# Unread matmuls in TensorE's waits: convolution, norms and one renumbered PSUM bank in a three-layer network

## The reference

```python
def first_block(...):
    for l in range(2):
        mix = conformer_conv(x, ...) if l == 0 else diff_attention(x, k1, k2, v, ...)
        x = layer_norm(ALPHA * x + mix, ln_mix_g[l], ln_mix_b[l])
        ffn = grouped_moe(x, router_w, router_bias, moe_w_gate[l], moe_w_up[l], moe_w_down[l])
        x = layer_norm(ALPHA * x + ffn, ln_ffn_g[l], ln_ffn_b[l])

def second_block(...):
    h = concatenate([meta, x])
    xn = rms_norm(h, mix_pre_g); proj = xn @ w_in
    y_ssd = ssd_mixer(z, xbc, dt_raw, ...); y_sb = rms_norm(stick_breaking_attention(q, k, v), sb_norm_g)
    h = h + rms_norm(concatenate([y_ssd, y_sb]) @ w_out, mix_post_g)
    xn = rms_norm(h, ffn_pre_g); gu = xn @ w_up
    f = (gelu(causal_dwconv(gu[..., :D_FF])) * gu[..., D_FF:]) @ w_down
    return h + rms_norm(f, ffn_post_g)
```

## Time and profile before

| | us |
|---|---|
| median of 3 runs | 1390.86 |
| lowest and highest | 1387.32, 1391.38 |
| the profiled execution, its own time | 1388.31 |
| its span, first to last instruction | 1386.6 |
| PE busy | 1298.2 (94%) |
| PE weight loads busy | 811.8 (59%) |
| DVE, ACT busy | 385.9 (28%), 262.3 (19%) |
| mean granted clock of PE | 0.966 of full speed |

### The profile page before, as it was taken

One profiled execution on the slowest core, in us unless ns is written; L12 is line 12 of the kernel. 1 busy time (PEld: TensorE's weight loads), 2 busy tenths in 40 slices (PEclk: granted clock), 3 DMA queues, 4 the chain that ended last, 5 costly groups with the idle time before them and its releaser, 6 DMA issues.

```text
span 1386.6 us, 14928 instructions
## 1 busy us (share of the span) xinstructions
PE 1298.2 (94%) x6134; PEld 811.8 (59%) x6134; DVE 385.9 (28%) x851; ACT 262.3 (19%) x579; POOL 35.9 (3%) x62
## 2 busy tenths in 40 slices
PE   7989899999989998999989799999998978999997
PEld 6764444333446864533434288776776867888743
DVE  0014522111141444411211303466323122222101
ACT  1013311000111343200100221411435021000000
POOL 3110000000000000000000000000000000000000
PEclk9999899999999999999999999889999999999999
DMA  9980899999993062999999942212230251544320
GB/s 310 297 266 2 334 386 428 423 426 429 418 384 121 1 242 101 417 423 428 425 426 426 401 182 87 96 61 92 91 121 1 69 174 61 171 133 175 130 91 31
DMA packets 95086, 321.68 MB, mean 232 GB/s; under 512 B 10098, under 2 KB 47510, under 8 KB 80166
## 3 DMA queue, kind: packets, MB, share of 16 engines
q1 hardware_dynamic: 84368, 301.04, 56.0%
q10 hardware_dynamic: 8662, 12.27, 3.0%
q0 software_dynamic: 1984, 7.34, 1.3%
HBM read 316.30 MB, written 4.34 MB: 231 GB/s over the span
## 4 chain that ended last, share of the span: by engine, by line
PE 82%; DMA 9%; DVE 5%; ACT 2%; issue 1%; ACTq 0%; SPq 0%; DVEq 0%; POOLq 0%
PE psum L255 35%; PE psum L1565 12%; PE psum L1598 6%; PE psum L3071 5%; DMA ring<-in_moe_w_up 4%; DMA arena<-in_moe_w_up 4%; PE psum L2870 4%; PE psum L1608 3%; PE psum L623 2%; PE psum L909 2%; PE psum L741 2%; PE psum L1802 2%; PE psum L531 1%; PE psum L1767 1%; PE psum L1224 1%
## 5 line engine op out<-in xcount | busy, mean ns | idle before, releaser
L255 PE MATMUL psum<-xT,ring 128*128 128x256 f32 (+2 forms) x1792 | 409.0, 390 | 3.4 <-DMA ring<-in_a_w_pw 3.4
L255 PEld LDWEIGHTS psum<-xT,ring 128*128 128x128 f32 x1792 | 344.0, 193 | 63.7 <-issue 9.0
L1565 PE MATMUL psum<-ring,arena 128*64 128x512 f32 x672 | 186.1, 599 | 10.1 <-DMA arena<-in_moe_w_up 6.3
L1565 PEld LDWEIGHTS psum<-ring,arena 128*64 128x64 f32 x672 | 60.1, 138 | 100.7 <-issue 100.5
L1446 DVE TENSOR_TENSOR arena<-psum,arena 64x512 f32<-64x512 f32 x32 | 34.2, 1070 | 214.5 <-ACT arena L1509 214.5
L1598 PE MATMUL psum<-ring,arena 128*64 128x512 f32 x384 | 85.0, 595 | 1.3 <-ACT arena L1526 1.3
L3071 PE MATMUL psum<-ring,arena 128*128 128x512 f32 x176 | 75.7, 592 | 0.0
L1565 PE MATMUL psum<-arena 128*64 128x512 f32 x208 | 74.0, 610 | 0.0
L1509 ACT ACTIVATE arena<-psum 64x512 f32<-64x512 f32 x32 | 18.9, 591 | 268.6 <-PE psum L1565 268.6
L1608 PE MATMUL psum<-arena 128*128 128x512 f32 x128 | 59.5, 605 | 0.0
L3071 PEld LDWEIGHTS psum<-ring,arena 128*128 128x128 f32 x176 | 33.4, 190 | 41.7 <-issue 41.6
(11 more groups left out here) (355 smaller groups left out, 1303.6 us busy)
## 6 DMA issues: line engine op xcount, KB each, us to landing
ring<-in_moe_w_down SPq DMA_DIRECT2D x24, 2048.0 KB, 25.5
ring<-in_moe_w_up SPq DMA_DIRECT2D x22, 2048.0 KB, 21.2
ring<-in_moe_w_gate SPq DMA_DIRECT2D x20, 2048.0 KB, 23.1
ring<-in_w_in SPq DMA_DIRECT2D x11, 2048.0 KB, 22.2
ring<-in_w_up SPq DMA_DIRECT2D x22, 1024.0 KB, 7.7
arena<-in_moe_w_gate SPq DMA_DIRECT2D x6, 2048.0 KB, 26.9
ring<-in_w_down SPq DMA_DIRECT2D x5, 2048.0 KB, 7.8
ring<-in_a_w_pw SPq DMA_DIRECT2D x8, 1024.0 KB, 11.0
```

The source lines that it names most:

```text
L255: last = nc.tensor.matmul(dst, lhsT, rhs, start=(n == 0), stop=(n == len(pairs) - 1))
L1565: last = pe.matmul(bank(j)[part, :], tokens[:, k, side * SEATS:side * SEATS + SEATS], weights(u + n, k), start=(k == 0), stop=(k == KC - 1))
```

## The change

`keep_busy(dst, n)` issues n products of `ident` (128 x 128) with 256 columns of `vec` into a PSUM bank from which nobody reads them. It is called in eight places on PE: five products behind `shift_sum` and five ahead of mix0, both into bank 7; three at the start of each `route` into bank 4; and in the norms, into the bank that the transposes are about to take: six ahead of tile 2 in `project_and_turn`, three ahead of each tile in mix1, eight ahead of tile 1 in `ffn_norm0`, fourteen ahead of tile 0 in `pre_norm`, fifteen ahead of tile 1 and eight ahead of tile 0 in `mix_and_turn`. Nine products of `ident` with itself (128 columns) follow the first transposes of the program. In `project_out` the sum of squares of `sqT` moves from bank 4 to a job of its own, so that `w_out` has eleven jobs, every later bank number moves by one and the two halves of the meta rows stand in banks 0 and 1 in their natural order; ACT frees the job's bank with a no-op behind its own result.

```diff
-    ("sb_v", 16), ("w_out", 10),
+    ("sb_v", 16), ("w_out", 11),
...
+    def keep_busy(dst, n):
+
+        for _ in range(n):
+            nc.tensor.matmul(dst[:, 0:2 * P], ident[:, :], vec[:, 0:2 * P], start=True, stop=True)
+
+    def transposes_pe(first, tiles, src, ready=None, busy=None):
...
         for t in tiles:
             n = TILE_N[t]
+            if busy is not None and t in busy:
+                take_bank(j)
+                keep_busy(bank(j), busy[t])
             if ready is not None:
                 ready(t)
...
         def turn(j, t):
-            transposes_pe(j, (t,), lambda t: xhat[t - 1], lambda t: pe.wait_ge(normed, t))
+            transposes_pe(j, (t,), lambda t: xhat[t - 1], lambda t: pe.wait_ge(normed, t), {2: 6})
...
             block.tensor(lambda pe: transposes_pe(first, (1, 2), lambda t: xhat_ffn[t - 1],
-                                                  lambda t: pe.wait_ge(normed, t)))
+                                                  lambda t: pe.wait_ge(normed, t), {1: 8}))
...
             transposes_pe(FJ["conv_xT"], (1, 2), lambda t: x_nat[:, t, :])
+            for _ in range(9):
+                pe.matmul(psum[:, 2 * BANKS - 1, 0:P], ident[:, :], ident[:, :], start=True, stop=True)
...
                         shift_sum()
+                        keep_busy(psum[:, 2 * BANKS - 1, :], 5)
...
+            keep_busy(psum[:, 2 * BANKS - 1, :], 5)
             project_and_turn(FJ["mix0"], unit_at["pw2"], lambda k, t: conv[:, k, (t - 1) * P:t * P], normed[0],
...
         def _(pe):
+            keep_busy(psum[:, BANKS, :], 3)
             all_read_out(pe, J)
...
-                transposes_pe(FJ["mix1"] + 2 * t - 2, (t,), lambda t: xhat[t - 1], lambda t: pe.wait_ge(normed[2], t))
+                transposes_pe(FJ["mix1"] + 2 * t - 2, (t,), lambda t: xhat[t - 1], lambda t: pe.wait_ge(normed[2], t),
+                              {1: 3, 2: 3})
...
         rms_to_T("pre", "pre_xT", lambda t: x_nat[:, t, :], lambda t: xn[:, t, :], xT, "mix_pre_g_2",
-                 ready=lambda t: nc.scalar.wait_ge(normed[3], t) if t else None)
+                 ready=lambda t: nc.scalar.wait_ge(normed[3], t) if t else None, busy={0: 14})
...
-            products(psum[:, BANKS, NEED:L], [(ones[:, :], sqT[:, c, NEED:L]) for c in range(KC)]).then_inc(so_summed_mix_turned, 1)
+            take_bank(SO)
+            products(bank(SO)[:, NEED:L], [(ones[:, :], sqT[:, c, NEED:L]) for c in range(KC)]).then_inc(job_done, 1)
...
-            act.wait_ge(so_summed_mix_turned, MIX_TURNED)
-            act.activation(rms_b, psum[:, BANKS, NEED:L], ACT.Sqrt, bias=eps_cols[:, 1:2], scale=1.0 / D).then_inc(
+            job_ready(act, SO)
+            act.activation(rms_b, bank(SO)[:, NEED:L], ACT.Sqrt, bias=eps_cols[:, 1:2], scale=1.0 / D).then_inc(
                 std_ready, 1)
-            turned_in(FJ["w_out"], mixT)
+            act.wait_ge(std_ready, root)
+            act.nop().then_inc(bank_free[SO % BANKS], 1)
+            turned_in(SO + 1, mixT)
...
             for t in FFN_ORDER:
                 n = TILE_N[t]
+                if t in (0, 1):
+                    take_bank(T + 2 * count[t])
+                    keep_busy(bank(T + 2 * count[t]), 8 if t == 0 else 15)
                 pe.wait_ge(rms_scaled, base + 4 + count[t])
```

More of the change, by code:

```diff
@@ L517, in next_stage @@
         block.gpsimd(meet)
-    def transposes_pe(first, tiles, src, ready=None):
+    def keep_busy(dst, n):
+        for _ in range(n):
+            nc.tensor.matmul(dst[:, 0:2 * P], ident[:, :], vec[:, 0:2 * P], start=True, stop=True)
+    def transposes_pe(first, tiles, src, ready=None, busy=None):
         j = first
@@ L2072, in _, with rms_to_T @@
                                              ALU.mult, ALU.mult).then_inc(scaled, 1)
-    def rms_to_T(name, job_name, src, dst, dstT, gain, pe_first=None, act_between=None, ready=None):
+    def rms_to_T(name, job_name, src, dst, dstT, gain, pe_first=None, act_between=None, ready=None, busy=None):
         first = rms_count[0]
@@ L2080, in rms_to_T @@
             block.scalar(act_between)
-        block.tensor(lambda pe: transposes_pe(FJ[job_name], ALL, dst, lambda t: pe.wait_ge(rms_scaled, first + t + 1)))
+        block.tensor(lambda pe: transposes_pe(FJ[job_name], ALL, dst, lambda t: pe.wait_ge(rms_scaled, first + t + 1),
+                                              busy))
         @block.scalar
@@ L2890, in _ @@
             for t in (1, 2):
-                turn(1, t).then_inc(so_summed_mix_turned, 1)
+                turn(1, t).then_inc(mix_turned, 1)
             for half in range(2):
@@ L2895, in _ @@
                 for c in range(4):
-                    last = pe.transpose(bank(j)[0:META, c * P:c * P + P], mixT[:, 4 * (1 - half) + c, 0:META], ident[:, :])
+                    last = pe.transpose(bank(j)[0:META, c * P:c * P + P], mixT[:, 4 * half + c, 0:META], ident[:, :])
                 last.then_inc(job_done, 1)
@@ L2923, in mix_and_turn @@
         gain_cols = vec[:, VEC_COL["ffn_pre_g_2"] + 4:VEC_COL["ffn_pre_g_2"] + 8]
-        assert J % BANKS == BANKS - 1
+        assert J % BANKS == 0
         def mix_rows(t):
-            banks = psum[:, 0:BANKS:BANKS - 1, :] if t == 0 else psum[:, BANKS + 2 * (t - 1):BANKS + 2 * t, :]
-            return banks[0:TILE_N[t]]
+            at = 0 if t == 0 else BANKS + 2 * (t - 1)
+            return psum[0:TILE_N[t], at:at + 2, :]
         def halves(rows):
@@ L2965, in mix_squares @@
                 if t:
-                    act.wait_ge(so_summed_mix_turned, MIX_TURNED + t)
+                    act.wait_ge(mix_turned, t)
                 else:
```

11 lines of the change are left out of this document (5 added, 6 removed).

## The result

The kernel after is slower: 1393.51 us median (1386.66 to 1396.43, 18 runs) against 1388.28 us (18 runs) for the kernel before in the same comparison, ratio 1.0043 with a 95% interval of 1.0031 to 1.0055: 5.2 us by the medians, 6.0 us by the ratio. The forecast was 1385.5 us, faster. The profiled execution of the kernel after has a span of 1390.8 us, 4.2 us more than the one before.

The account below looks back on a forecast made before the run. PE is busy 94% of the span, so gains come only at its low clock or in waits on the path. Terms 0 - 1.7 - 2.9 - 1.9 + 4.1 + 0 + 2.0 - 4.2 = -4.6 us; forecast 1385.5 us, range 1377 to 1392.

Parts of the forecast that it names:

- the start: Nine products before the first weights: 1.7 us gained, then lost at taps(5)'s wait for rows; 0, bounds -1.8 and +4.
- the start turns: Rival: PE's earlier start brings an expert's load forward, delaying rows for taps(4) and taps(5); +4 us, 1389 to 1391; chance 0.17.
- shift_sum: Five products fit the 2.7 us wait before taps(5), whose instructions then run at full clock: -1.7 us, kept.
- mix0: Five products in 2.60 us of idle time; seven following instructions run at full clock: -2.9 us, kept.
- route0: Nine products in layer 0's waits for norm and router hold the clock over L1224: -1.9 us, bounds -2.5 and 0.
- pre_norm: Fourteen products behind a long second overflow test, four at low clock; z begins later: +2.0 us, bounds +3.5 and -1.6.
- ffn_norm0: Eight products start only after PE's own long overflow test, half at low clock: +4.1 us, bounds +5.8 and -2.2.
- Both tests' length: PE's overflow tests before ffn_norm0 and pre_norm: both assumed long, 6.1 us, though the second was 0.36 us before.
- mix_and_turn: Fifteen and eight products in the last norm, full clock into ffn: -4.2 us, bounds -4.6 and -3; project_out's new banks 0.
- mix1, route1: Three groups of three products in layer 1's waits; about 1 us gained but loads already queued: 0, bound -1.0.
- Both tests short and one short: Rivals on PE's overflow tests: both short, 1374 to 1376 us, chance 0.08; only one short, 1378 to 1382, chance 0.12.
- Products by the identity not holding the clock: Rival: every filler costs, about +17, 1405 us; chance 0.05; sign: the clock falls within a run of them.

Follow-up runs that it names:

- a_no_start: Kernel after without the nine products at the start: 0.9976, 1384.28 us.
- a_no_tests: Kernel after without the eight products of ffn_norm0 and the fourteen of pre_norm: 0.9994, 1386.71 us.
- b_out: Kernel before with only the last part of the change: project_out's new job and banks, mix_and_turn's 23 products: 0.9965, 4.1 us less.
- a_late4: Kernel after, whole, with the four experts' loads issued during the convolution moved behind taps(4): 0.998, 1384.78 us.
- y4: Kernel before plus four loads moved behind taps(4), nine start products, mix0's five, pre_norm's fourteen, project_out and mix_and_turn part: 0.9888, 1372.38 us.
- y2: Kernel before plus four loads moved behind taps(4), nine start products, pre_norm's fourteen, project_out and mix_and_turn part: 0.987, 1371.23 us.

## Why the prediction was wrong

**The step that failed first** is the start: "PE comes earlier to a wait whose end is set by traffic. I take 0, with bounds of -1.8 (all kept) and +4". In the kernel after it costs 4.1 us by the table at the first product of mix0 and 4.1 to 4.9 by a_no_start, at or beyond that upper bound. (Of the 7.0 us of the lag at `taps(5)`, 5.2 are there when `taps(4)` begins; its low clock adds 2.4 and the products behind `shift_sum` 2.3, and the old wait of 2.7 us ahead of `taps(5)` is gone.) The rival "the start turns" had the place, the mechanism and the size; it was given 0.17. What spoke for it was in the trace that the forecast had: `taps(5)` waited 2.73 us and `taps(4)` 1.08 us, and the engines were saturated. Loads that are asked for at other times don't leave a wait beside them where it is: the small transfers share the engines with them packet by packet and move back. The view of the transfers of 70 to 80 us, with 14.6 us for 144 KB, would have shown how much was at stake; the forecast had not priced the rows' way.

**The second step** is that the gains of shift_sum, mix0 and route0 (-6.5 us) "come before the transfers of the experts start, so they are kept". The pair of traces agrees with each of the three terms within 0.4 us, and would have passed for proof. The medians don't: of the 5.2 us by which the kernel is slower, the start makes +4.1, the products of the two tests +6.8 (a_no_tests), the last part -4.1 (b_out), which leaves -1.6 us for everything else (0.0 if all but the start is taken from the ratios), uncertain by 3 us, where the forecast had -6.5. The other traces show where the 6.5 us are lost, and it is on PE itself and not in the transfers. From the first product of moe0 to its last group it takes 218.4 us on average without these products and 218.2 us with them.

- **shift_sum.** Its products need a wait ahead of `taps(5)`. In six of the seven traces with them that wait was gone, in the kernel after too, and they cost their 2.3 us. And `taps(5)` ran at the low clock in three of the twelve traces without them only; in the other nine it took 3.66 us, and there was nothing to win.
- **mix0.** It takes 28.6 us at the full clock, in all traces with the products. In the ten traces with neither these nor route0's it took 28.6 to 31.5 us, 30.1 on average. So 1.6 us are won, not 2.9: the trace of before, with 31.46, is among the longest.
- **route0.** The products do hold the clock over the router and the residual sums (4.4 us in place of 5.0 to 6.7). But PE then waits 1.7 us for the winners, the clock falls next, and the 32 products that gather the experts' tokens run low instead. In the ten traces without the products they take 3.81 us each time, in six of the seven with them 5.3 to 6.7 us; only the trace of the kernel after kept the clock. From the last product of mix0 to the first of moe0 it took 20.0 to 21.6 us without (21.1 on average) and 20.1 to 23.1 us with them (22.1). The forecast of -1.9 us is +1.0.

The gather in before, then in a_late4, with the row of that stretch. The clock is 0.54 over it, and 1.00 over the residual sums from 148.2 to 152.6 us; in before it is the other way round, 1.00 and 0.54:

```profile
166.21 3.81 PE L255 MATMUL psum<-arena 128*128 128x128 f32 x32 [0.94 <-issue]
```

```profile
156.51 6.74 PE L255 MATMUL psum<-arena 128*128 128x128 f32 x32 [0.94 <-issue]
...
156.50:163.20 6.70, 6.69 (x34) 6.58 (x34) 1.04 (x6) 1.88 (x2) 0.00 (x0) 0.54 1.01 397
```

From mix0's first product to the last group of moe0 it took 269.7 us on average in the ten traces without (268.4 to 270.9) and 268.9 us in the seven with (266.1 to 270.3); the trace of the kernel after has the 266.1, that of before the 270.9. So of 4.8 us forecast in that stretch about 0.7 reached the end of moe0, and the agreement of the pair was luck. No run has route0's products alone.

**pre_norm** was right in its mechanism, a long second test, and short in its size: +4.0 us against +2.0, 0.5 beyond its upper bound. The products took 8.74 us, not 7.7, since the clock was low for the first 5 us of them, and z began 3.9 us behind the transposes' start, not 3.0.

**ffn_norm0** was right: forecast +4.1, +4.4 in the traces, with the products behind the test and partly at the low clock. Its reason, that the products stand in a wait that is PE's own test and not the norm's, is borne out by a_no_tests. **Both tests' length** was forecast as it came out, by a choice and not by a rule: the forecast had no places. Measured by place behind a multiple of 256, tests were short at 4, 11, 15, 24 and from 219 to 251 and long at 40, 51, 112, 116, 148 and 195.

**mix_and_turn** and the new bank numbers: forecast -4.2 and 0, measured -4.1 and 0.

**mix1, route1**: forecast 0. From attention to the last group of moe1 0.3 us less; not tried alone.

**Rivals.** Both tests short and one short: neither occurred. Products by the identity not holding the clock: the clock was full at 115.8, 153.4 and 1146.7 us. Its sign, a fall within a run of them, did come all the same: in ffn_norm0 the clock fell 0.9 us into the products, at 397.2 us, behind 4.31 us in which PE had stood idle. So the sign was too weak to tell the case.

## What to carry to other kernels

Work put into a wait pays only if the wait would be there without it and is ended by someone else: ask which engine ends it, and whether the filler stands before or behind what really holds the engine. A wait for a small transfer beside large ones is a question of what shares its queues' packets; moving four large loads out of its way by one line was worth 8 us here, where all the fillers of the change together lost 5, and it turned a loss of 4.1 us at the start into a gain of 2.1. A clock that is held over one stretch may fall in the next gap instead, over work that had run at the full clock: look at what runs behind. And a trace of one execution that agrees with a term within 0.4 us doesn't show that the term is kept at the end; compare a later point over several runs.

## What the runs showed of the hardware that was not expected

Where a branch stands in the program decides whether it takes 0.33 to 0.47 us or 6.1 us: 24 instructions on a semaphore that was already up, at the very start, made layer 0's short. Behind a short one PE may still stand for 1.8 to 2.3 us after 8 to 12 matmul instructions (a_no_start, y4), or 0.25 us after 18 (y2), until the same 6.1 to 6.2 us behind the branch's start are over. And two queues share the engines by packets, not bytes: 244 packets each in 10 us, 3.60 MB against 0.24 MB.
